# A PEER decoder layer on one core: the gate table built by indirect DMA in device memory instead of by one-hot matmuls

## The reference, cut to what matters

```python
s1 = einsum('thd,nd->thn', qh[..., :half], sub_keys_1); s2 = ...   # 8 heads, 128 + 128 sub-keys
v1, i1 = top_k(s1, 16); v2, i2 = top_k(s2, 16)
top_s, top_j = top_k(cand, 16)                       # 16 of the 256 sums of each head
experts = take_along_axis(i1 * 128 + i2, top_j)      # (256 tokens, 8 * 16)
gate = softmax(top_s)                                # over the 16 of a head
a = gelu(einsum('cd,ced->ce', x, expert_u[experts]))
y = einsum('ce,ced->cd', gate * a, expert_v[experts])
```

## Time and profile before

| | |
|---|---|
| median of 3 runs | 1075.41 us (1075.36 to 1076.88) |
| span of the profiled execution | 1075.6 us |
| mean granted TensorE clock | 0.965 of full speed |
| PE busy | 1043.2 us (97%) |
| DVE, ACT, POOL busy | 750.1, 436.2, 106.7 us |
| bytes read and written | 174.33 MB, 1.05 MB |
| PE on the chain that ended last | 94% |

### The profile page before, as it was taken

The page is one execution under the profiler, slowest core; times in us unless marked ns, Lnnn a source line. Parts: engine busy times, 40 slices in busy tenths (PEclk is TensorE's granted clock), DMA queues, the critical chain, the costliest instruction groups (busy, mean ns, idle before and its releaser), DMA issues.

```text
span 1075.6 us, 17382 instructions
## 1 busy us (share of the span) xinstructions
PE 1043.2 (97%) x6508; PEld 914.9 (85%) x6508; DVE 750.1 (70%) x1818; ACT 436.2 (41%) x769; POOL 106.7 (10%) x210
## 2 busy tenths in 40 slices
PE   7998988999999999999999999989999999999996
PEld 3477855879999999999999999988888888888885
DVE  1173157348999968999999986556666666666667
ACT  1243223323344475555555544443333333333341
POOL 1000000000300023333333320000000000000000
PEclk9999568899999999999999999999999999999998
DMA  9733100337355554444444445556555655555551
GB/s 333 302 157 137 40 0 1 106 130 273 138 178 184 188 178 142 146 144 140 138 139 138 141 144 176 191 188 229 191 193 194 195 196 195 193 191 192 193 190 39
DMA packets 48610, 176.50 MB, mean 164 GB/s; under 512 B 5120, under 2 KB 6160, under 8 KB 47248
## 3 DMA queue, kind: packets, MB, share of 16 engines
q1 hardware_dynamic: 48128, 173.82, 47.7%
q0 software_dynamic: 400, 1.58, 0.4%
HBM read 174.33 MB, written 1.05 MB: 163 GB/s over the span
## 4 chain that ended last, share of the span: by engine, by line
PE 94%; DVE 4%; DMA 1%; ACT 1%; issue 0%; SPq 0%; DVEq 0%
PE ps L447 92%; PE ps L616 1%; DMA arena<-in_w_tok 1%; DVE slab L1215 0%; DVE arena L1316 0%; PE ps L682 0%; DVE xs L1618 0%; DVE xs L1612 0%; DVE arena L1606 0%; SPq L346 0%; DVE xs L1603 0%; PE ps L517 0%; DVE arena L1242 0%; ACT arena L951 0%; ACT arena L934 0%
## 5 line engine op out<-in xcount | busy, mean ns | idle before, releaser
L447 PE MATMUL ps<-x1hl,hi 128*128 128x256 f32 x2216 | 377.7, 285 | 0.0
L447 PEld LDWEIGHTS ps<-x1hl,hi 128*128 128x128 f32 x2216 | 327.3, 192 | 0.0
L447 PE MATMUL ps<-hi,ahl 128*128 128x512 f32 x992 | 266.5, 390 | 3.0 <-DVE lo L1577 3.0
L447 PEld LDWEIGHTS ps<-hi,ahl 128*128 128x128 f32 x992 | 187.1, 189 | 42.1 <-issue 3.1
L1108 ACT CAST hi<-slab 128x1024 fp32r<-128x1024 f32 x128 | 134.4, 1052 | 207.0 <-PE ps L447 206.8
L447 PE MATMUL ps<-x1hl,lo 128*128 128x256 f32 x688 | 194.6, 283 | 0.0
L1577 DVE TENSOR_TENSOR lo<-slab,hi 128x1024 fp32r<-128x1024 f32 x128 | 155.8, 1217 | 0.0
L447 PE MATMUL ps<-lo,ahl 128*128 128x512 f32 x496 | 153.3, 390 | 0.0
L447 PEld LDWEIGHTS ps<-x1hl,lo 128*128 128x128 f32 x688 | 131.7, 191 | 0.0
L447 PE MATMUL ps<-arena 128*128 128x128 f32 (+6 forms) x800 | 119.9, 310 | 1.4 <-ACT arena L934 0.7
L1359 DVE TENSOR_TENSOR lo<-slab,hi 128x1024 fp32r<-128x1024 f32 x86 | 105.9, 1232 | 14.1 <-ACT hi L970 14.0
(11 more groups left out here) (199 smaller groups left out, 846.0 us busy)
## 6 DMA issues: line engine op xcount, KB each, us to landing
slab<-in_pv SPq DMA_DIRECT2D x128, 512.0 KB, 4.3
slab<-in_uT SPq DMA_DIRECT2D x107, 512.0 KB, 3.4
arena<-in_wq SPq DMA_DIRECT2D x32, 512.0 KB, 4.7
ahl_raw<-in_uT SPq DMA_DIRECT2D x21, 512.0 KB, 3.2
arena<-in_w_tok SPq DMA_DIRECT2D x2, 2048.0 KB, 16.5
arena<-in_w_out SPq DMA_DIRECT2D x1, 4096.0 KB, 13.5
arena<-in_w_tok SPq DMA_DIRECT2D x4, 512.0 KB, 8.4
arena<-in_w_tok SPq DMA_DIRECT2D x1, 1792.0 KB, 19.0
```

Of the source, the lines that this page charges most:

```text
L447: return nc.tensor.matmul(o, lhsT, rhs, start=start, stop=stop, skip_group_check=True)
```

## The change

The one-hot matrices, their matmuls, the turning of the routes, the ones in `arena` and the groups on DVE all go. In their place:

- A table `gates` of 128 x 128 x 256 floats (16.8 MB: expert, token) lies in device memory. SP writes zeros over it with 8 DMAs of 2 MB out of an SBUF tile `zeros` of 1 KB a partition, behind the first 7 loads of the query weights.
- `route(t)` ends with one instruction for the address (expert * 256 + token) and, now within it, the softmax. POOL then issues 128 indirect DMAs for each t, one for each slot of the 8 x 16: each adds 128 floats (one for each token) at 128 addresses of the table. Before each head but the first it waits until all earlier ones of that t have landed.
- In the second products SP loads block c of the table (128x256, 128 KB, rows of 1 KB) into a ring of 8 (`gring`), and DVE multiplies it into `arena` two blocks ahead of its use (`gate_block`).
- The gelu of every block goes straight to `arena`. The ring of `expert_v` has 6 places and not 8.
- The start of the second products is spread: two blocks of `expert_v` load into places that are free after the routes, and `v_split(0)` to `(3)` and `a_split(0)` wait for the end of first products 125 to 128 (`pe_h`) one by one, not for all of them.
- The second exponential of the routes comes after gelu 27, the first before gelu 0; both came after gelu 32.

```diff
-VR, VH = 8, 4
+VR, VH = 6, 4
+GR = 8
+AHEAD = 2
+ZERO_DMAS = 8
...
+        gring = slab[:, 4096:6144].rearrange("p (b n) -> p b n", b=GR)
+        zeros = sb("zeros", [P, S])
+        gates = nc.dram_tensor("gates", [NK, P, S], F32, kind="Internal").ap()
+        gates_flat = gates.rearrange("c p t -> (c p t)").unsqueeze(1)
...
         def v_slot(c):
-            return (c + 4) % VR
+            return (6, 7, 2, 3, 0, 1)[c % VR]
+        def v_hi_slot(c):
+            return (3, 2, 0, 1)[c % VH]
...
             for j in range(RING):
                 load_query(j)
+            sp.wait_ge(zero_ready, 1)
+            n = NK // ZERO_DMAS
+            for c in range(0, NK, n):
+                sp.dma_start(gates[c:c + n].rearrange("c p t -> p c t"),
+                             zeros[:, :].unsqueeze(1).to_broadcast([P, n, S])).then_inc(zeroed, 16)
...
-            for c in range(NK):
+            def load_v(c):
                 if c == 0:
-                    sp.wait_ge(pe_g, GN)
-                elif 4 <= c < VR:
-                    sp.wait_ge(pe_h, NK)
+                    sp.wait_ge(route_ready, T)
+                elif 2 <= c < VR:
+                    sp.wait_ge(pe_h, (NK - 5, NK - 4, NK - 1, NK)[c - 2])
                 elif c >= VR:
                     sp.wait_ge(pe_y, c - VR + 1)
                 sp.dma_start(raw[:, v_slot(c), :], pv[c]).then_inc(v_in[c % VR], 16)
+            def load_gates(c):
+                if c == 0:
+                    for t in range(T):
+                        sp.wait_ge(scattered[t], 16 * PH * TK)
+                if c >= GR:
+                    sp.wait_ge(gated, c - GR + 1)
+                sp.dma_start(gring[:, c % GR, :], gates[c]).then_inc(g_in[c % GR], 16)
+            load_v(0)
+            load_v(1)
+            for c in range(GR):
+                load_gates(c)
+            for c in range(NK):
+                if c + 2 < NK:
+                    load_v(c + 2)
+                if c + GR < NK:
+                    load_gates(c + GR)
...
-            pool.wait_ge(rT_saved, T)
-            onehots(0)
-            onehots(1)
...
+            def scatter(t, head):
+                if head:
+                    pool.wait_ge(scattered[t], 16 * TK * head)
+                for k in range(TK):
+                    s = head * TK + k
+                    pool.indirect_dma_start(
+                        gates_flat, bass.IndirectOffsetOnAxis(slot_at[:, t, s:s + 1], 0),
+                        slot_gate[:, t, s:s + 1], None, compute_op=ALU.add).then_inc(scattered[t], 16)
+            pool.wait_ge(zeroed, 16 * ZERO_DMAS)
+            for t in range(T):
+                pool.wait_ge(route_ready, t + 1)
+                for head in range(PH):
+                    scatter(t, head)
...
             for c in range(NK):
-                if c == NTURN:
-                    turn_routes()
-                if 0 <= c - N0 < GN:
-                    gates(c - N0)
                 expert_in(c)
...
-            pe.wait_ge(pre_gated, GN)
             for c in range(NK - NT):
                 expert_out(c)
...
+            def v_split(c):
+                act.wait_ge(v_in[c % VR], (c // VR + 1) * 16)
+                if c < VH:
+                    act.wait_ge(pe_h, NK - 3 + c)
                 else:
+                    act.wait_ge(pe_y, c - VH + 1)
+                nc.scalar.copy(hi[:, v_hi_slot(c), :], raw[:, v_slot(c), :]).then_inc(v_hi, 1)
...
+                if c == 27:
+                    route_exp(1)
+                if c >= NK - VH:
+                    v_split(c - NK + VH)
...
+            def gate_block(c):
+                dve.wait_ge(g_in[c % GR], (c // GR + 1) * 16)
                 dve.wait_ge(gelu_done, c + 1)
                 a = arena[:, c * S:(c + 1) * S]
-                v.tensor_tensor(a, gel[:, c % 2, :], a, ALU.mult).then_inc(gated, 1)
+                v.tensor_tensor(a, gring[:, c % GR, :], a, ALU.mult).then_inc(gated, 1)
...
             def a_split(c):
+                dve.wait_ge(gated, c + 1)
                 if c == 0:
-                    dve.wait_ge(pre_gated, GN)
-                    dve.wait_ge(gated, NK - N0)
-                    dve.wait_ge(pe_h, NK)
+                    dve.wait_ge(pe_h, NK - 2)
...
+            for c in range(AHEAD):
+                gate_block(c)
             for c in range(NK):
                 a_split(c)
                 v_rest(c)
+                if c + AHEAD < NK:
+                    gate_block(c + AHEAD)
```

More of the change, by code:

```diff
@@ L243, in peer_layer_kernel @@
               rawf[:, 2048:4096].rearrange("p (i a s) -> p i a s", i=4, a=2)]
-        ocs = [oh[:, 1 - t, :, :, :].rearrange("p a b c -> p (a b c)") for t in range(T)]
+        ocs = [slab[:, 4096 + 1024 * (1 - t):5120 + 1024 * (1 - t)] for t in range(T)]
         ghk = ar(A_CX, 32)
@@ L302, in peer_layer_kernel @@
         g_shift, g_exp, route_ready = sem("g_shift"), sem("g_exp"), sem("route_ready")
[L303 to L306, removed]
+        zeroed, scattered = sem("zeroed"), [sem(f"scattered{t}") for t in range(T)]
+        zero_ready = sem("zero_ready")
+        g_in = [sem(f"g_in{b}") for b in range(GR)]
         u_in = [sem(f"u_in{b}") for b in range(UR)]
@@ L1079, in fill_ones, with route_exp @@
-            def fill_ones(part):
-                n = 2048
-                at = A_R + part * n
-                if part == 0:
-                    act.wait_ge(one_ready, 1)
-                nc.scalar.copy(arena[:, at:at + n], one.to_broadcast([P, n])).then_inc(ones_mid, 1)
+                if c == NK // 2:
+                    act.wait_ge(route_ready, T)
+                nc.scalar.activation(arena[:, c * S:(c + 1) * S], ps[:, c % 2, 0:S], ACT.Gelu).then_inc(gelu_done, 1)
+            def route_exp(t):
+                act.wait_ge(g_shift, t + 1)
+                nc.scalar.activation(te[:, t], te[:, t], ACT.Exp).then_inc(g_exp, 1)
@@ L1089, in _ @@
                     u_split(c + UH)
[L1090 to L1110 removed]
+                if c == 27:
+                    route_exp(1)
+                if c >= NK - VH:
+                    v_split(c - NK + VH)
+            for c in range(VH, NK):
                 v_split(c)
@@ L1511, in _ @@
             route(1)
-            for t in range(T):
-                dve.wait_ge(g_exp, t + 1)
-                did(v.tensor_reduce(gs[:, 0:PH], te[:, t], AX_X, ALU.add))
-                settle()
-                did(v.reciprocal(gs[:, PH:2 * PH], gs[:, 0:PH]))
-                settle()
-                v.tensor_tensor(ex[:, t, 2, :].rearrange("p (h k) -> p h k", h=PH), te[:, t],
-                                gs[:, PH:2 * PH].unsqueeze(2).to_broadcast([P, PH, TK]), ALU.mult
-                                ).then_inc(route_ready, 1)
@@ L1547, in block_gate @@
-            def block_gate(c, groups):
+            assert filled[0] == NROUTE
+            while filled[0] < NK:
+                fill()
+            def gate_block(c):
+                dve.wait_ge(g_in[c % GR], (c // GR + 1) * 16)
                 dve.wait_ge(gelu_done, c + 1)
-                if groups:
-                    dve.wait_ge(pre_gated, groups)
-                else:
-                    dve.wait_ge(ones_low, 1)
                 a = arena[:, c * S:(c + 1) * S]
-                v.tensor_tensor(a, gel[:, c % 2, :], a, ALU.mult).then_inc(gated, 1)
```

178 lines of the change are left out of this document (26 added, 152 removed).

## The result

The changed kernel takes 1285.39 us (median of 4 runs, 1280.17 to 1288.1) against 1076.12 for the kernel before on the same chip: a ratio of 1.194, 95% interval 1.191 to 1.196. The forecast was 1013, with a range from 1008 to 1145. The profiled execution took 1280.17 us, its span is 1278.4. The case that came is rival C, slower, but by more than its upper bound of 1166.

The account below looks back on a forecast made before the run. PE was taken as the bound, with 94% of the chain. 1075.6 - 57.4 (first products) - 2.95 (PE's wait) - 1.9 (slow first block) = 1013.4, less 0.2 for the median: 1013 us, range 1008 to 1145.

Parts of the forecast that it names:

- rival C: POOL's chain becomes the bound from 1.44 us a scatter, its issue held by DVE's fills: 1116 to 1166 us; chance 0.27.
- I take 1.1 for one, the middle: Price of one indirect DMA on POOL: 1.1 us, between 0.55 and 1.60, putting the last addition's landing at 624 us.
- 1.60 for each: Upper price of an indirect DMA on POOL: 0.55 for a direct issue plus 1.05 from a compute instruction's worst case.
- X: Time when POOL's last addition to the table has landed: forecast 624 us, at most 651 if PE is not held.
- A: The forecast itself: POOL's additions stay hidden behind PE's first products; 1013 us, own range 1008 to 1021; chance 0.46.
- B: Additions partly late: above 1.21 us an indirect DMA, PE waits before the second products; 1046 us at 1.33; chance 0.17.
- The waits between heads: On POOL, 14 waits between heads and one at the end, 3 us each: 45 us in all.
- PE, first products: On PE, all 128 blocks at 2.88 us, ending at 656.0 instead of 713.4: 57.4 us less.
- The change of phase: Between first and second products, PE's wait of 2.95 us and the slow first block's 1.9 us go.
- Second products: DVE's gates and the added loads cost nothing: blocks stay at 2.72 us, DVE's wait falls from 0.83 to about 0.4.
- rival D: Writing the table's zeros at 150 GB/s makes the first norm 32 us late: 1045 us; chance 0.04.
- the cover: Time in which POOL's indirect DMAs stay hidden behind PE's first products: 354 us, from 297 to 651.

Follow-up runs that it names:

- the one-input fill: The changed kernel with the low parts of expert_u made by a DVE copy of the raw block instead of a subtraction: 1199.6 us (one run).
- the run with 96 scatters: The changed kernel with six scatters a head instead of 16, so 96 indirect DMAs and not 256: 1014.41 us, ratio 0.9426.

## Why the prediction was wrong

**The step that failed** is "I take 1.1 for one, the middle", and with it the upper bound, "1.60 for each". Bare, a scatter occupies POOL for 1.54 + 0.30 = 1.85 us, and beside fills for 2.88; the mean over all, with the gaps and without the waits between heads, is (495.6 + 87.0) / 256 = 2.28. The threshold above which the change loses was worked out as 1.44. The bounds came from a direct DMA's 0.55 us and a compute instruction's worst case; neither is kin to an indirect DMA of 128 rows, and the runs put its three parts at: the instruction with its rows 0.96, adding 0.58, the gap 0.30. The gap was in no term at all, though it is 72 us in sum, and 87 with the six long pauses. Even a bare plain scatter (1.26 with its gap) lies above the 1.21 that the forecast could bear.

**Rival C's mechanism** was right and its size was not. POOL is held while DVE fills: by the kernel's rows 101 us in sum, and 83 of them are gone with the one-input fill (the scatters' busy time fell from 495.6 to 412.4). I let a fill of 1.2 us shut POOL out, which made 1.44 of 1.1; in fact 1.54 became 2.58, longer by 1.04. The measured time follows from C's own formula with the real X: 1013 + (912 - 651) + 2 = 1276, against 1280 in the profiled run. The Trainium skill ("SBUF — State Buffer", section "Who interferes with whom") says that `tensor_tensor` with two SBUF inputs contends with GpSimd's reads only, and infers that the writing of descriptors does not stall beside it. Here a scatter beside exactly such an operation takes 2.58 instead of 1.54 us, so for this indirect DMA the measurement decides against that comfort. Whether it is the reading of its 128 addresses from SBUF that is held, no run shows.

**Rivals A and B** had 0.63 of the chance on a price for which no row stood. With ends at 0.55 and 1.60 for an operation not in the trace, the middle was no estimate: the nearest row by kind (an instruction of POOL over 128 rows, 0.60 us, plus a DMA's issue of 0.55, 1.15 in sum) lay just under B's threshold of 1.21, and whatever DVE adds came on top. The range's top of 1145 lay inside C's upper end of 1166, and so took a guess for a bound.

**The waits between heads** were taken too long, which hid 12 us of the miss: 45 us forecast for 15 of them, measured 31.9 for the 14 between heads and 1.5 behind the last scatter, 33 in sum. One DMA lands 3.0 us after its start, as taken, but 1.54 of that is the scatter's own time on POOL; a wait costs POOL 1.7 to 1.8 us where nothing else runs, and up to 4.2 beside the first products. The Trainium skill's fixed 2.0 us ("DMA: Bandwidth & Descriptors", section "Anatomy of one DMA — SWDGE (gpsimd) path") gave 30 for them in the prediction, which is nearer; from the start of a scatter to its landing it is 1.0 too short.

**PE, first products:** right. They run from 285.46 to 654.3, 368.9 us, whole at a clock of 1.00, and the run with 96 scatters shows the sum, 1014 against 1013.

**The change of phase:** right as a part (4 to 5 us in its own run, 4.85 forecast); in the changed kernel the gap there is 263 us, and the granted clock is 0.50 in it and 0.70 behind it.

**Second products:** right. DVE's wait went from 0.83 to 0.50, blocks stayed at 2.72; from PE's restart to the end it is 361.4 us against 359.2; the 2.2 us were not followed up.

**The zeros** (rival D): right. The zeros ran at 354 GB/s at 90 to 95, where 210 were needed, and the first norm began at 173.79, not late against 175.22:

```profile
L1276 DVE SCALAR_TENSOR_TENSOR xs<-xs,ps x4: 672/683/689, 173.8 to 241.9; 128x512 f32<-128x512 f32 x4
```

## What to carry to other kernels

Before many indirect DMAs are put on GpSimd, count instructions and not bytes or rows: each costs about 1.3 us when it writes and 1.85 when it adds, for 128 rows of one element and hardly less for 64. And a bound for an operation that the trace does not hold must come from the same kind of work; where the verdict hangs on it (here 1.44 us against a guess of 1.1), the honest range reaches well past the worst row at hand. A chain on an idle engine is free only while its whole length, gaps and waits with it, fits under the cover: 256 x 2.4 us, waits included, did not fit under 354.

## What the runs showed of the hardware

- An indirect DMA of 128 one-element rows holds POOL for 0.96 us, adding for 1.54, and the next begins 0.30 later. With 64 rows: 0.90 and 1.41.
- An adding scatter makes one packet for each row and 16 more (144 with 128 rows, 80 with 64), a plain one 32 with either; that is 37264 packets in the kernel against 8592. With nothing but adding scatters running the DMA share is 0.22 (665 to 905), so the DMA engines are far from full and POOL is the limit.
- A 128x1024 `tensor_tensor` of DVE with two SBUF inputs, 1.23 us, lengthens a scatter that it meets by 1.04 us; a one-input copy of the same size, 0.70 us, by up to 0.5. DVE's own time is not changed (1.22 to 1.23 us).
- While POOL issues plain scatters PE can be left with one instruction in 1.40 us, or none for 16 to 21 us, at a granted clock of 0.50 and with the DMA engines at a share of 0.02. In the profiled executions, adding scatters did it in none of four, plain ones in nine of thirteen. What PE lacks there stays open.
